# Two f32 networks on one Trainium2 core: selections two tasks later, mLSTM maxima through device memory, pooled means in two products, zeros multiplied during the first loads

## What is computed

```python
# mLSTM, one head: decay weights with a running maximum
dmat = jnp.where(tri, bc[..., :, None] - bc[..., None, :] + ic[..., None, :], -jnp.inf)
m_t = jnp.maximum(a, jnp.max(dmat, axis=-1))
p = jnp.einsum('bhcld,bhcsd->bhcls', qc, kc) * jnp.exp(dmat - m_t[..., None])

# mixing layer: sparse attention, the 64 best keys of each query
q = apply_rope(rms_norm(q, q_g), cos, sin)
k = apply_rope(rms_norm(k, k_g), cos, sin)
score = jnp.einsum('bqhs,bqh->bqs', jax.nn.relu(sc), iwb) * (IDX_HEADS ** -0.5)
_, idx = lax.top_k(score, top_k)          # top_k = 64

# mixing layer: pooled means over windows of 2, 4, 8, 16 tokens
means.append((c - lagged) / cnt)
pooled = jnp.stack(means, axis=2) - ug
```

## Time and profile before

| | |
|---|---|
| median of 3 runs | 1549.44 us (1547.89 to 1549.5) |
| the profiled execution, its own time | 1549.4 us |
| its span, first to last instruction | 1547.5 us |
| PE busy | 1531.9 us (99%) |
| VectorE, ScalarE, GpSimd busy | 65%, 52%, 23% |
| PE's waits that are put down to VectorE's splits (line 938) | 3.0 us in 4 |
| mean transfer rate | 192 GB/s |

### The profile page before, as it was taken

The page is one execution under the profiler, slowest core; times in us unless marked ns, Lnnn a source line. Parts: engine busy times, 40 slices in busy tenths (PEclk is TensorE's granted clock), DMA queues, the critical chain, the costliest instruction groups (busy, mean ns, idle before and its releaser), DMA issues.

```text
span 1547.5 us, 18966 instructions
## 1 busy us (share of the span) xinstructions
PE 1531.9 (99%) x7227; PEld 1269.0 (82%) x7227; DVE 1002.4 (65%) x1223; ACT 806.6 (52%) x1008; POOL 349.7 (23%) x371
## 2 busy tenths in 40 slices
PE   8999999999999999999999999999999999999999
PEld 6788888888888888888878888887788888778887
DVE  5656576666655656466666665569966666996664
ACT  5544455465444544466766444466375446637542
POOL 2342010013420344000001442013541100354110
PEclk9999999999999999999999999999999999999999
DMA  9865763167557674664436755664645456464543
GB/s 303 249 210 170 251 214 134 64 219 233 184 193 256 197 222 151 205 226 164 163 126 222 221 185 192 210 242 154 211 139 177 177 185 252 155 204 144 177 173 126
DMA packets 261222, 297.05 MB, mean 192 GB/s; under 512 B 80381, under 2 KB 174757, under 8 KB 261152
## 3 DMA queue, kind: packets, MB, share of 16 engines
q1 hardware_dynamic: 258880, 289.11, 56.7%
q0 software_dynamic: 2128, 6.97, 1.4%
q10 hardware_dynamic: 144, 0.03, 0.0%
HBM read 277.20 MB, written 1.06 MB: 180 GB/s over the span
## 4 chain that ended last, share of the span: by engine, by line
PE 86%; DVE 8%; ACT 2%; issue 2%; POOL 1%; DMA 1%; SPq 0%; DVEq 0%; ACTq 0%; POOLq 0%
PE ACC L938 22%; PE ACC L931 22%; PE ACC L932 22%; DVE WL L2218 2%; PE ACC L1125 2%; PE ACC L1127 2%; PE ACC L1126 2%; PE ACC L1225 1%; PE ACC L859 1%; PE ACC L1227 1%; PE ACC L1226 1%; PE ZB L1095 1%; PE TB L956 1%; PE TB L968 1%; PE ACC L1015 1%
## 5 line engine op out<-in xcount | busy, mean ns | idle before, releaser
L2218 DVE TENSOR_TENSOR WL<-RAW,WH 128x2048 fp32r<-128x2048 f32 (+2 forms) x256 | 518.9, 2067 | 198.1 <-ACT WH L1498 197.2
L1498 ACT ACTIVATE WH<-RAW 128x2048 fp32r<-128x2048 f32 (+3 forms) x254 | 419.2, 1698 | 158.5 <-PE ACC L938 98.5
L931 PE MATMUL ACC<-WH,XH 128*128 128x512 f32 (+2 forms) x1272 | 491.3, 387 | 1.1 <-ACT WH L1498 0.8
L932 PE MATMUL ACC<-WH,XL 128*128 128x512 f32 (+2 forms) x1272 | 488.2, 385 | 0.0
L938 PE MATMUL ACC<-WL,XH 128*128 128x512 f32 (+2 forms) x1272 | 334.8, 385 | 3.0 <-DVE WL L2218 3.0
L931 PEld LDWEIGHTS ACC<-WH,XH 128*128 128x128 f32 x1272 | 238.9, 188 | 51.9 <-issue 2.0
L938 PEld LDWEIGHTS ACC<-WL,XH 128*128 128x128 f32 x1272 | 235.9, 188 | 52.0 <-DVE WL L2218 4.7
L932 PEld LDWEIGHTS ACC<-WH,XL 128*128 128x128 f32 x1272 | 239.0, 188 | 46.4
L2091 POOL COPY HID<-TURNED 128x512 uint16<-128x512 uint16 x88 | 112.7, 1324 | 166.7 <-DMA TURNED<-PLANES 166.7
L1602 ACT ACTIVATE SIDE<-ACC,RX 128x256 f32<-128x256 f32 x88 | 41.1, 473 | 204.5 <-PE ACC L938 204.4
L931 PE MATMUL ACC<-WH,HH 128*128 128x512 f32 x352 | 137.3, 390 | 0.0
(11 more groups left out here) (345 smaller groups left out, 1976.4 us busy)
## 6 DMA issues: line engine op xcount, KB each, us to landing
RAW<-w_in_in SPq DMA_DIRECT2D x66, 1024.0 KB, 6.6
RAW<-ffn_w_gate_in SPq DMA_DIRECT2D x42, 1024.0 KB, 5.1
RAW<-ffn_w_up_in SPq DMA_DIRECT2D x42, 1024.0 KB, 7.5
RAW<-ffn_w_down_in SPq DMA_DIRECT2D x32, 512.0 KB, 4.4
RAW<-ffn_w_down_in SPq DMA_DIRECT2D x16, 1024.0 KB, 7.1
RAW<-mlstm_w_in_in SPq DMA_DIRECT2D x16, 1024.0 KB, 6.3
RAW<-ffn_w_down_in SPq DMA_DIRECT2D x16, 768.0 KB, 6.0
RAW<-attn_w_in_in SPq DMA_DIRECT2D x12, 1024.0 KB, 7.1
```

What stands on the lines that cost most here:

```text
L931: nc.tensor.matmul(bank, lh, wh[:, i, :], start=first and i == 0, stop=False)
L932: nc.tensor.matmul(bank, ll, wh[:, i, :], start=False, stop=False)
L1498: nc.scalar.activation(WH[:, slot, lo:hi], RAW[:, slot, lo:hi], ACT.Copy).then_inc(hi_ready, 1)
L2218: nc.vector.tensor_tensor(WL[:, slot, lo:hi], RAW[:, slot, lo:hi], WH[:, slot, lo:hi].bitcast(F32), ALU.subtract).then_inc(lo_ready, 1)
```

## The change

1. *Selections.* `select 0 1` goes from slot 12 (between the head sums and the rotation of the keys) to slot 14, `select 1 0` from 14 to 15. `select 0 0` (11) and `select 1 1` (16) stay.
2. *mLSTM maxima.* The three products per head go, and with them IDR, AFR, MUH and MUL on VectorE and ScalarE. GpSimd stores MU (8 x 256) to device memory, loads it back spread over the partitions for two heads at a time (256 KB each) into two tiles MASKED, and adds the causal mask; `decay` reads MASKED. `weighted` now also waits for the scores.
3. *Pooled means.* The constants are laid so that the first tile's 128 columns and the 16 columns of its neighbour stand side by side: one product of 144 columns and one of 128.
4. *Zeros.* VectorE clears part of HL; PE multiplies it into ZB eight times before it waits for the identity, and eight times more before the first product. The bank is written over later.

```diff
-        tiles.append(np.concatenate([inside / np.minimum(t + 1, w) - (s == t), inside / w - (s == t), near / w], axis=1))
+        tiles.append(np.concatenate([inside / np.minimum(t + 1, w) - (s == t), near / w, inside / w - (s == t)], axis=1))
...
-        task(12, ("norms", "k"), ("select", 0, 1), ("rotate", "k"))
-        task(14, ("select", 1, 0))
+        task(12, ("norms", "k"), ("rotate", "k"))
+        task(14, ("select", 0, 1))
+        task(15, ("select", 1, 0))
         task(16, ("select", 1, 1))
...
                 if at.stage == 0:
                     of_x(0, t)
+                    zeros_into(ZB, 8)
...
-                    if h == 0:
-                        pe.wait_ge(largest_lo, 1)
...
-                        nc.tensor.matmul(z[:, t], QK[:, HEADS + h, t], QK[:, h, t], start=True, stop=True)
-                    m = z[:, SEQ:2 * SEQ]
-                    of_head = IDR[:, h:h + 1].broadcast_to([P, P])
-                    nc.tensor.matmul(m, of_head, MUL[:, :], start=True, stop=False)
-                    nc.tensor.matmul(m, of_head, MUH[:, :], start=False, stop=False)
-                    nc.tensor.matmul(m.rearrange("p (c t) -> p c t", c=2), IDR[:, :],
-                                     AFR[:, :].unsqueeze(1).broadcast_to([P, 2, P]), start=False, stop=True).then_inc(z_ready, 1)
+                        ins = nc.tensor.matmul(z[:, t], QK[:, HEADS + h, t], QK[:, h, t], start=True, stop=True)
+                    ins.then_inc(z_ready, 1)
...
-                            nc.tensor.matmul(bank[:, 0:P], u[0], PM[:, g, 0:P], start=True, stop=True)
-                            nc.tensor.matmul(bank[:, P:SEQ], u[1], PM[:, g, P:2 * P], start=True, stop=False)
-                            mm = nc.tensor.matmul(bank[:, P:P + WINDOWS[-1]], u[0], PM[:, g, 2 * P:], start=False, stop=True)
+                            near = P + WINDOWS[-1]
+                            nc.tensor.matmul(bank[:, 0:near], u[0], PM[:, g, 0:near], start=True, stop=False, skip_group_check=True)
+                            mm = nc.tensor.matmul(bank[:, P:SEQ], u[1], PM[:, g, near:], start=False, stop=True, skip_group_check=True)
...
+            def zeros_into(bank, n):
+
+                for i in range(n):
+                    nc.tensor.matmul(bank[:, :], HL[:, 2, 0:P], HL[:, 0:2, :].rearrange("p k n -> p (k n)"), start=i == 0, stop=i == n - 1)
+
             pe.sem_inc(weights_used, 1)
+            pe.wait_ge(zeros_set, 1)
+            zeros_into(ZB, 8)
             pe.wait_ge(ident_loaded, 16)
...
-                    act.wait_ge(gates_dve, 4)
-                    nc.scalar.activation(MUH[:, :], MU[:, :], ACT.Copy).then_inc(largest_hi, 1)
...
-                    act.wait_ge(z_ready, u0 + h + 1)
+                    act.wait_ge(largest_masked, h // 2 + 1)
...
-                                                   (ZB, OB)[h % 2][:, SEQ + c * P:SEQ + (c + 1) * P], ACT.Exp,
+                                                   MASKED[h // 2 % 2][:, h % 2, c * P:(c + 1) * P], ACT.Exp,
...
+                def spread(half):
+
+                    if half:
+                        pool.wait_ge(w_ready, 2 * HEADS + 4)
+                    for i in range(2):
+                        of_two = bass.AP(tensor=largest_dram.tensor, offset=(4 * half + 2 * i) * SEQ, ap=[[0, P], [SEQ, 2], [1, SEQ]])
+                        pool.dma_start(MASKED[i][:, :, :], of_two).then_inc(largest_spread, 16)
+                    pool.wait_ge(largest_spread, 32 * (half + 1))
+                    for i in range(2):
+                        m = MASKED[i][:, :, :].rearrange("p h (c t) -> p (h c) t", c=NTOK)
+                        nc.gpsimd.tensor_tensor(m, m, after.unsqueeze(1).broadcast_to([P, 2 * NTOK, P]), ALU.add).then_inc(largest_masked, 1)
+
+                pool.wait_ge(gates_dve, 4)
+                pool.dma_start(largest_dram, MU[0:HEADS, :]).then_inc(largest_stored, 16)
+                pool.wait_ge(largest_stored, 16)
+                spread(0)
+                spread(1)
...
                     dve.wait_ge(w_ready, u0 + h + 1)
+                    dve.wait_ge(z_ready, u0 + h + 1)
...
+            nc.vector.memset(HL[:, 0:3, :].bitcast(F32), 0.0).then_inc(zeros_set, 1)
```

More of the change, by code:

```diff
@@ L211, in program @@
         o += HEADS * (P + 1) * 4
+        decay_at = (o + 31) // 32 * 32
+        o = decay_at + 2 * SEQ * 4
         assert o <= top[0]
@@ L248, in program @@
         CT = sb("CT", list(c_tiles.shape))
[L249 to L252, removed]
+        MASKED = [sb(f"MASKED{i}", [P, 2, SEQ], offset=at) for i, at in enumerate((decay_at, sbuf_at["CT"] + C_PAST * 4))]
         SS = sb("SS", [P, 4])
@@ L347, in program @@
         assert top[0] <= nc.sbuf_usable_end, (top[0], nc.sbuf_usable_end)
+        largest_dram = nc.dram_tensor("largest_by_head", (HEADS, SEQ), F32, kind="Internal").ap()
         bias_dram = nc.dram_tensor("bias_by_distance", (HEADS, 3 * P), F32, kind="Internal").ap()
@@ L406, in program @@
         mixed = sem("mixed")
-        largest_hi = sem("largest_hi")
-        largest_lo = sem("largest_lo")
+        largest_stored = sem("largest_stored")
+        largest_spread = sem("largest_spread")
+        largest_masked = sem("largest_masked")
         left_ready = sem("left_ready")
@@ L420, in program @@
         hidden_lo = sem("hidden_lo")
+        zeros_set = sem("zeros_set")
         second_turned = sem("second_turned")
@@ L2510, in mlstm @@
                 nc.vector.memset(VA[:, :, :, P:P + 1], 1.0)
-                step(nc.vector.memset(MU[:, :], 0.0))
-                step(nc.vector.tensor_copy(IDR[:, :], ident))
-                step(nc.vector.tensor_copy(AFR[:, :], after))
                 prenorm()
@@ L2584, in exps @@
                     step(nc.vector.tensor_scalar(WI[:, :], EX[:, H:2 * H], P ** -0.5, None, ALU.mult))
-                    dve.wait_ge(largest_hi, 1)
-                    nc.vector.tensor_tensor(MUL[:, :], MU[:, :], MUH[:, :].bitcast(F32), ALU.subtract).then_inc(largest_lo, 1)
                 def weighted(h):
                     dve.wait_ge(w_ready, u0 + h + 1)
+                    dve.wait_ge(z_ready, u0 + h + 1)
                     z = (ZB, OB)[h % 2][:, 0:SEQ].rearrange("p (c t) -> p c t", c=NTOK)
```

## The result

| kernel | median us | runs | ratio to before (95% interval) |
|---|---|---|---|
| before | 1549.44 (1547.09 to 1550.73) | 21 | |
| changed | 1551.07 (1549.6 to 1555.89) | 21 | 1.0016 (1.001 to 1.0021) |

What follows compares the result with a forecast made beforehand. TensorE, busy for 99% of the span, was taken as the bound. Selections +6.5, mLSTM maxima -1.5, pooled means -1.6 and zeros -0.7 gave +2.7 us on 1549.4, so 1552.1 us; the range ran from 1549.5 to 1557.0.

Steps and rivals of the forecast that it cites:

- wait for chunk 8 stays: Mixing layers: the keys' rotation still waits for GpSimd's power HR, so PE's 1.5 us wait at 1089 us stays; gain 0.0.
- new waits in block cb: Both mixing layers: block cb's weight split comes 3.5 us late, PE loses 3.4 and 3.1 us; +6.5, between +6.0 and +7.6.
- clock after them: PE behind the new waits in block cb: the forecast's sum held no clock loss; only a rival did.
- rival C: PE's clock falls in block cb's new gap, 2.2 us per block: 1556.5 us, or 1554.3 if once; chance 0.12.
- the three others: mLSTM maxima -1.5 us, pooled means -1.6 and zeros at the start -0.7: together -3.8 us.
- order on VectorE: First mixing layer: split, first tile's maxima, product, second tile's first half, then block cb's split at 1103.5 us, 3.5 late.
- Rival A: Keys' rotation follows the head sums without waiting for HR, removing 3.0 us of waits: 1542.6 us; chance 0.10.
- Rival B: GpSimd's power HR takes half its 2.9 us when VectorE is idle: 1546.6 us; chance 0.06.
- Rival D: The mLSTM maxima spread through device memory come late, ScalarE starting at 737.8 instead of 728.05: about 1560 us; chance 0.04.
- estimate of 725.1 us: mLSTM: store, loads and GpSimd's additions end at 725.1 us, before the first exponential, right behind the table at 728.05.
- heads 0 and 1 give nothing: mLSTM: head 2's scores wait for ScalarE's table load chain, so heads 0 and 1's 0.7 us becomes a longer wait.
- 0.11 us a pass: Pooled means: six passes take 0.67 us per group; four passes would take 0.47, giving -1.6 us over eight groups.

Runs made afterwards that it cites:

- kept busy: The changed kernel with twelve more unused products on PE while it waits for block cb's weights in both mixing layers: 1549.33 us, ratio 1.0004.
- old order: The changed kernel with the selections put back where they were before the change: 1543.35 us, ratio 0.9965; a second time 1543.32 us, 0.9960.
- mLSTM kernel: The kernel before with only the mLSTM maxima sent through device memory: 1546.64 us, ratio 0.9983.

## Why the prediction was right, and where it was so by two errors

It gave 1552.1 us and the time is 1551.07. Its steps one by one:

| step | forecast us | measured us | from |
|---|---|---|---|
| wait for chunk 8 stays | 0.0 | 0.0 | stand of 1.71 at 1085.41 |
| new waits in block cb | +6.5 (3.4 and 3.1) | 5.6 (3.24 and 2.33); 6.0 in medians | rows; kept busy against old order |
| clock after them | 0 (rival C: 2.2 each) | 4.6 in the trace; 1.7 in medians | rows; kept busy against changed |
| the three others | -3.8 | -6.0 (-5.3 by the lengths of stages) | old order against before |
| sum | +2.7 | +1.6 | |

*The order on VectorE* was right where it was worked out: 1103.5 less the 4.45 us by which everything is earlier is 1099.05, and the second split begins at 1099.03 us. In the second layer it was sized too high. VectorE there, before and now:

```profile
1370.77 5.43 DVE L2218 TENSOR_TENSOR WL<-RAW,WH 128x2048 fp32r<-128x2048 f32 x2
```
```profile
1370.19 0.28 DVE L2758 TENSOR_TENSOR IS<-IS,CT 128x128 f32<-128x128 f32 x1
...
1374.44 4.91 DVE L2238 TENSOR_TENSOR WL<-RAW,WH 128x2048 fp32r<-128x2048 f32 x2
```

The split starts at 1374.44 us; less 0.82 that is 2.85 behind 1370.77 of before, not 3.5. The second tile's first half, with the short operation IS<-IS,CT ahead of it, takes 4.25 us (1370.19 to 1374.44), where it took 4.66 in both layers of before and takes 4.78 in the first layer now. The difference is the short operation: 0.28 us instead of 0.69 (before, both layers) and 0.80 (first layer now). In the kernel with the selections alone it is the other way round, 0.28 us in the first layer and 0.81 in the second, and its stands are 3.02 and 3.47 us. The split then takes 4.91 us for both halves where it took 5.43, which is the other half microsecond. GpSimd was copying beside the operation in all these places; what decides its length was not tried.

*Rival A fell.* Chunk 8's wait stayed, because VectorE stood for the power: [3.42 <-POOL HR L2169]. *Rival B fell*: the power took 2.90 us with VectorE idle, as before. *Rival D fell*: the store went out at 704.91 us, the loads 4.3 us behind it, and the two additions ran from 713.97 to 717.65, 7.5 us before the first exponential at 725.19:

```profile
704.91 0.58 POOL L2134 DMA_DIRECT2D largest_by_head<-MU  x1 [14.11 <-DVE DG L2589]
709.79 1.12 POOL L2127 DMA_DIRECT2D MASKED<-largest_by_head  x2 [4.29 <-DMA largest_by_head<-MU]
713.97 3.68 POOL L2131 TENSOR_TENSOR MASKED<-MASKED,CT 128x512 f32<-128x512 f32 x2 [3.07 <-DMA MASKED<-largest_by_head]
```

The estimate of 725.1 us, built from the DMAs of the position bias, was too late by 4.5 (717.65 + 2.95, by which this stage starts earlier, is 720.6). The loads made most of it: 256 KB each, they landed 3.3 to 3.5 us after their issue, where the prediction took the 7.3 us of a load of 1024 KB; the store, 8 KB, took 4.6 where one of 12 KB took 5.4.

*Rival C came true, beside the forecast and not instead of it.* This was the step that failed: I gave it 0.12 and left it out of the sum. A stand of 3.42 us, which the forecast itself drew, did bring 1.2 GHz back, and in the first layer for longer than supposed, 2.85 us lost rather than 2.2 (1.7 in the second). The median carries 1.7 for both layers where the profiled execution lost 4.6. The Trainium skill ("TensorE: Matmul & The Clock Gate", What you observe, and the states below it) has idle time bring the half rate back. The runs agree that it is the idling; they show besides that the fall does not go by length alone (below).

*The three others gave 2.2 us more than forecast.* The maxima (-1.5 in the length of their stage) and the pooled products (1.5 us by their rows, 1.8 by the lengths of the two mixing stages, 1.6 forecast) are as worked out, including the step that heads 0 and 1 give nothing: head 2's wait grew from 0.3 to 1.2 us. (The forecast's 0.11 us a pass is an average: of the 0.67 us of a group before, the two narrow passes take 0.15 and the two behind them 0.30, and what goes with the narrow product is the same 0.2.) So most of the excess sits in the start. The zeros were sized by the second token tile's transposes, at 14.0 instead of 14.76. They came at 13.30. Of that, 0.7 us come from the weights: ScalarE began the third quarter at 11.09 us instead of 11.76, and this varies from execution to execution without any zeros, too (11.76, 10.73, 11.66 and 11.58 us in the four profiles without them; 11.09, 10.76, 11.18, 10.63 and 11.74 in five with them). What the zeros themselves change is the distance from that quarter to the transposes: 3.0, 2.6, 2.5 and 3.1 us without, 2.2 in all five with them, a gain of 0.6 on average and so close to the 0.7 forecast. Taking half of them away costs 1.4 us, though, and zeros alone bring 2.1 in the median (-0.5 to -3.3). The second stage says the same as these two: its first transposes come at 191.4, 191.1, 189.0 and 189.5 us in the four profiles without zeros, 190.3 on average, and at 187.8 to 189.6 in the nine with all sixteen, 188.6 on average, 1.6 us sooner. The third stage is another 0.4 us shorter with them (181.7 us in all nine, 181.9 to 182.2 in the four). That makes 2.0 us for the zeros where 0.7 were forecast, uncertain by some 0.7 since each profile is one execution. The row that the forecast looked at, the second tile's transposes, does not hold all of the gain; which waits give the rest is open.

So the net was right, within 1.1 us, and partly by luck: the clock was not counted (+1.7) and the three others, the start above all, were counted too low (-2.2), while the waits were counted 0.5 us too high. The mechanism of the waits was right; two errors of some two microseconds beside it had opposite signs.

## What to carry to other kernels

Before a task is moved away from in front of a wait, read what that wait's other operands were doing: a task that fills another engine's latency is free, and moving it makes it cost its full length wherever it lands. If it must go, put in its place work that a busier engine wants soon; here that turned the new order of the selections from 7.7 us slower than the old one into one no slower (its median is 2 us lower with the second tile's halves moved too, 0.9939 to 0.9966 of before against 0.9947 to 0.9974, which overlap). And count a stand of TensorE of some 3 us higher than its length: behind it the matmuls may run at half speed for several microseconds, which a few dummy products in the stand prevent.

## What the runs showed of the hardware that I had not expected

- The clock fell in the changed kernel at stands of 3.42 and 2.95 us from start to start, and in the kernel with the selections alone at one of 3.02. In the same execution of the latter it did *not* fall at a longer one, in the second mixing layer. Its PE rows there, and the window behind it, with the clock at 1.00:

```profile
1377.46 0.39 PE L933 MATMUL ACC<-WH,XL 128*128 128x512 f32 x1
1380.93 1.20 PE L939 MATMUL ACC<-WL,XH 128*128 128x512 f32 x4 [3.08 <-DVE WL L2219]
```
```profile
1382.00:1386.00 4.00, 4.00 (x19) 3.33 (x18) 3.79 (x11) 2.28 (x2) 3.77 (x4) 1.00 0.43 124
```

  3.47 us without a fall and 2.95 with one: the length of the stand is not all that decides. No stand of 1.7 us or less in the mixing blocks brought it down in any profile, while at the start, with the clock just up, it fell 1.7 us after a wait of 1.51. The fall differs between executions of one kernel: the mean granted clock of the changed kernel's 21 reads from 1.000 to 0.996.
- The fall can show late: with the selections alone PE restarted at 1105.24 us at full pitch and went to 0.43 us only from 1106.64 on; in the changed kernel's first layer the clock was down within the stand, and PE was slow from the restart.
- The start of the program differs by up to 2.4 us between executions of kernels that are the same there: the mLSTM kernel, with no zeros, reached its second stage at 189.0 us and the kernel before at 191.4. A part judged by a single total can hide in that. The stages behind it repeat closely where the program is the same: 139.28 to 139.34 us for the mLSTM stage in the four profiles with the old maxima, 137.75 to 137.82 in the eight with the new, so a part is better judged by its stage.
